# First layer's r projection as Strassen's seven products, behind q and k, with the weight-block sums formed in DRAM

## What is computed

```python
q, k, v, r, g_low = jnp.split(x @ w_in, [GLA_HK, 2 * GLA_HK, 2 * GLA_HK + GLA_HV, 2 * GLA_HK + 2 * GLA_HV], axis=-1)
log_a = jax.nn.log_sigmoid((g_low @ w_gate_up + b_gate).astype(f32)) / GLA_TAU
...
cum = jnp.cumsum(to_chunks(log_a, GLA_DK), axis=3)
q_dec = q * jnp.exp(cum); k_inv = k * jnp.exp(-cum); k_end = k * jnp.exp(total - cum)
a = jnp.where(causal, jnp.einsum('bhcid,bhcjd->bhcij', q_dec, k_inv), 0.0)
...
o = ((o - mu) * lax.rsqrt(var + LN_EPS)).reshape(B, S, GLA_HV) * norm_g.astype(f32)
y = jax.nn.silu(r.astype(f32)) * o
return y.astype(x.dtype) @ w_out
```

## Time and profile before

| What | Value |
|---|---|
| Median of 3 runs | 1132.15 us |
| The profiled execution | 1132.14 us |
| Its span | 1130.4 us |
| TensorE (PE) busy | 1120.2 us, 99% |
| Weight loads (PEld) | 994.7 us |
| VectorE (DVE) busy | 784.6 us |
| ScalarE (ACT) busy | 569.8 us |
| POOL busy | 325.6 us |
| Mean granted TensorE clock | 0.999 |

### The profile page before, as it was taken

The page is one execution under the profiler, slowest core; times in us unless marked ns, Lnnn a source line. Parts: engine busy times, 40 slices in busy tenths (PEclk is TensorE's granted clock), DMA queues, the critical chain, the costliest instruction groups (busy, mean ns, idle before and its releaser), DMA issues.

```text
span 1130.4 us, 18412 instructions
## 1 busy us (share of the span) xinstructions
PE 1120.2 (99%) x6828; PEld 994.7 (88%) x6828; DVE 784.6 (69%) x1263; ACT 569.8 (50%) x926; POOL 325.6 (29%) x215
## 2 busy tenths in 40 slices
...
GB/s 227 167 150 112 112 38 149 13 271 164 273 279 211 245 182 175 234 197 170 108 112 75 95 47 94 48 150 75 38 191 279 237 248 280 214 74 298 189 193 75
DMA packets 34459, 183.35 MB, mean 162 GB/s; under 512 B 3152, under 2 KB 7376, under 8 KB 20704
## 3 DMA queue, kind: packets, MB, share of 16 engines
...
...
## 4 chain that ended last, share of the span: by engine, by line
PE 96%; DVE 1%; issue 1%; DMA 1%; ACT 0%; POOL 0%; SPq 0%; DVEq 0%; POOLq 0%; ACTq 0%
PE bank L2057 29%; PE bank L2059 29%; PE bank L2058 29%; PE bank L2509 2%; PE bank L2493 2%; PE bank L2140 1%; PE bank L2088 1%; PE bank L2530 1%; PE bank L2529 1%; DMA s_raw<-stream 1%; PE bank L2338 1%; DVE s_w_lo L1330 1%; PE bank L2331 0%; PE bank L2346 0%; PE bank L2324 0%
## 5 line engine op out<-in xcount | busy, mean ns | idle before, releaser
L2057 PE MATMUL bank<-s_t_hi,s_w_hi 128*128 128x256 f32 (+1 forms) x832 | 264.4, 318 | 0.0
L2058 PE MATMUL bank<-s_t_lo,s_w_hi 128*128 128x256 f32 (+1 forms) x832 | 262.8, 316 | 0.0
L2059 PE MATMUL bank<-s_t_hi,s_w_lo 128*128 128x256 f32 (+1 forms) x832 | 262.8, 316 | 0.0
L1179 POOL TENSOR_TENSOR s_w_lo<-s_raw,s_w_hi 128x1024 fp32r<-128x1024 f32 x64 | 160.1, 2512 | 180.3 <-ACT s_w_hi L638 180.3
L638 ACT ACTIVATE s_w_hi<-s_raw 128x1024 fp32r<-128x1024 f32 x107 | 111.3, 1057 | 114.6 <-PE bank L2059 90.5
L2059 PEld LDWEIGHTS bank<-s_t_hi,s_w_lo 128*128 128x128 f32 x832 | 158.6, 191 | 10.2
L2057 PEld LDWEIGHTS bank<-s_t_hi,s_w_hi 128*128 128x128 f32 x832 | 158.7, 191 | 9.7 <-issue 0.2
L2058 PEld LDWEIGHTS bank<-s_t_lo,s_w_hi 128*128 128x128 f32 x832 | 158.7, 191 | 9.4
L1216 POOL TENSOR_TENSOR s_w_lo<-s_raw,s_w_hi 128x512 fp32r<-128x512 f32 x36 | 67.2, 1866 | 274.3 <-ACT s_w_hi L768 274.3
L2057 PE MATMUL bank<-s_t_hi,s_w_s_hi 128*128 128x256 f32 x432 | 122.4, 283 | 0.0
L2059 PE MATMUL bank<-s_t_hi,s_w_s_lo 128*128 128x256 f32 x432 | 122.2, 283 | 0.0
...
## 6 DMA issues: line engine op xcount, KB each, us to landing
s_raw<-stream SPq DMA_DIRECT2D x75, 1024.0 KB, 4.8
sums<-down POOLq DMA_DIRECT2D x12, 2816.0 KB, 20.9
s_more_raw<-sums SPq DMA_DIRECT2D x12, 1024.0 KB, 4.9
sums<-sums POOLq DMA_DIRECT2D x4, 2816.0 KB, 12.9
s_raw<-down SPq DMA_DIRECT2D x8, 1024.0 KB, 4.9
s_ln_gb<-ln_gb ACTq DMA_DIRECT2D x4, 1024.0 KB, 7.0
s_more_raw<-down SPq DMA_DIRECT2D x4, 1024.0 KB, 7.5
s_raw<-sums SPq DMA_DIRECT2D x4, 1024.0 KB, 4.9
```

The lines of the kernel that those rows point to most:

```text
L1179: nc.gpsimd.tensor_tensor(lo, raw_pair(SLOTS[place // 2])[:, n % 2, cols], hi.bitcast(F32), ALU.subtract).then_inc(lo_done, new)
L2057: nc.tensor.matmul(out, l_hi, r_hi, start=start, stop=False, skip_group_check=skip)
L2058: nc.tensor.matmul(out, l_hi, r_lo, start=False, stop=False, skip_group_check=skip)
L2059: return nc.tensor.matmul(out, l_lo, r_hi, start=False, stop=stop, skip_group_check=skip)
```

## The change

The order becomes v (slabs 0 to 7), q and k (8 to 15), r (16 to 29) and the output projection (30 to 37). r's 8 blocks of work become 7 products of half the tokens, half the depth and half the columns, numbered from 0; each takes two slabs, 24 matmuls. Four of the seven need sums of weight blocks: POOL issues eight transfers between its low parts of slabs 5 to 19. Sums of x are made by VectorE after the gate weights' rows, with high parts on ScalarE and low parts on VectorE behind the copies of v; a fourth one after product 2. The q and k of heads 0 and 1 are copied to SBUF by ScalarE and scaled from there. The products go into four pairs of banks, and ScalarE's copies and VectorE's additions put r's quarters together before SiLU and gain. VectorE takes r's low parts from slab 20 on. x and the layer-norm gains are loaded after product 5. Semaphores of the gate are merged.

```diff
-GLA_R = GLA_V + KD
-GLA_QK = GLA_R + KD
-GLA_OUT = GLA_QK + 2 * GLA_HEADS
+GLA_QK = GLA_V + KD
+GLA_R = GLA_QK + 2 * GLA_HEADS
+GLA_OUT = GLA_R + 2 * 7
...
+qk_raw = sb_at("qk_raw", [P, 2, 2, SEQ], F32, rg_at)
+r_ops = [halves_at(f"r_op{i}", [P, KD // 2, SEQ // 2], at_, at_ + 4 * KB)
+         for i, at_ in enumerate((h_at, h_at + 8 * KB, gb_at))]
...
 MIDDLE = P // 2 - 1
-EARLY_R = 3
+EARLY_QK = 3
+R_BANKS = {"x": (0, 1), "y": (4, 5), "z": (6, 7), "w": (2, 3)}
+R_QUARTERS = ((0, 0), (1, 0), (0, 1), (1, 1), (2, 1), (3, 1), (2, 0), (3, 0))
...
+        if GLA_R <= n < GLA_OUT:
+            p = (n - GLA_R) // 2
+            if p in SUM_READY:
+                sp.wait_ge(r_blocks, 16 * SUM_READY[p])
+            array, which = SOURCES[p]
+            sp.dma_start(raw_pair(slot).rearrange("p a c -> p (a c)"), a["r_" + array][which]).then_inc(raw_full[slot], 16)
+            continue
...
+    for i in range(3):
+        act.wait_ge(r_op_sum, i + 1)
+        nc.scalar.activation(r_ops[i]["hi"][:, :, :], r_ops[i]["sum"][:, :, :], ACT.Copy).then_inc(r_op_hi, 1)
     act.wait_ge(low_done, 1)
...
-    for n in range(GLA_R, GLA_R + EARLY_R):
+    def copy_qk(hd, is_k):
+        act.wait_ge(slab_done, GLA_QK + 2 * hd + is_k + 1)
+        nc.scalar.activation(qk_raw[:, hd, is_k, :], bank[4 + 2 * hd + is_k][:, :], ACT.Copy).then_inc(qk_copied, 1)
+    for n in range(GLA_QK, GLA_QK + EARLY_QK):
         split_hi(n + RING)
-    act.wait_ge(centred_cum, 1)
+    for hd in range(2):
+        for is_k in range(2):
+            copy_qk(hd, is_k)
+    split_hi(GLA_QK + EARLY_QK + RING)
+    act.wait_ge(gate_steps, 1)
...
-                split_hi(n + RING)
-        for t in range(TILES):
-            if t < TILES - 1:
-                act.wait_ge(tok_done[1], half * (TILES - 1) + t + 1)
-            else:
-                act.wait_ge(slab_done, GLA_R + (half + 1) * (KD // 2))
-            nc.scalar.activation(g_rg[:, t, half * HALF:(half + 1) * HALF],
-                                 bank[4 - 4 * half + t][:, :], ACT.Silu).then_inc(tok_out[1], 1)
-    for n in range(GLA_QK, GLA_OUT - 1):
-        split_hi(n + RING)
+    def r_split(first, end):
+        for slab in range(first, end):
+            split_hi(GLA_R + slab)
+    def r_done(p):
+        act.wait_ge(slab_done, GLA_R + 2 * p + 2)
+    def r_copy(b, quarter):
+        t, half = R_QUARTERS[quarter]
+        nc.scalar.activation(g_rg[:, t, half * HALF:(half + 1) * HALF], bank[R_BANKS[b][t % 2]][:, :],
+                             ACT.Copy).then_inc(r_copied, 1)
+    def r_silu(quarter):
+        t, half = R_QUARTERS[quarter]
+        act.wait_ge(r_merged, quarter + 1)
+        nc.scalar.activation(g_rg[:, t, half * HALF:(half + 1) * HALF], g_rg[:, t, half * HALF:(half + 1) * HALF],
+                             ACT.Silu).then_inc(tok_out[1], 1)
+    r_split(0, 5)
+    r_done(0)
+    act.wait_ge(qk_scaled, 6)
+    r_copy("x", 0)
+    r_copy("x", 1)
+    r_split(5, 8)
+    r_silu(0)
+    r_silu(1)
+    r_split(8, 9)
+    r_done(2)
+    act.wait_ge(r_op_sum, 4)
+    nc.scalar.activation(r_ops[0]["hi"][:, :, :], g_rg[:, 2:4, 0:HALF].rearrange("p t (k c) -> p t k c", k=2),
+                         ACT.Copy).then_inc(r_op_hi, 1)
+    r_copy("y", 4)
+    r_copy("y", 5)
+    r_split(9, 11)
+    r_done(3)
+    r_copy("x", 2)
+    r_copy("x", 3)
+    r_split(11, 14)
+    for n in range(GLA_OUT, GLA_OUT + 2):
+        split_hi(n)
+    r_silu(2)
+    r_silu(3)
+    r_done(5)
+    act.dma_start(h[:, :, :], a["x"].rearrange("(t p) d -> p t d", p=P)).then_inc(h_full, 16)
+    load_gb(0)
+    act.wait_ge(r_op_lo, 4)
+    r_copy("x", 6)
+    r_copy("x", 7)
+    r_silu(4)
+    r_silu(5)
+    split_hi(GLA_OUT + 2)
+    r_silu(6)
+    r_silu(7)
     def ke_tile_out(t):
         act.wait_ge(ke_turned, t + 1)
...
     nc.gpsimd.memset(keep[:, :].rearrange("p (t i) -> p t i", i=P)[:, :, 0:1], 0.0).then_inc(consts, 1)
     pool.wait_ge(lo_done, RING)
+    def r_block_sum(step):
+        to, array, which = SUM_STEPS[step]
+        if step:
+            pool.wait_ge(r_blocks, 16 * step)
+        if step % 2:
+            nc.gpsimd.dma_start(a["r_sums"][to], a["r_" + array][which], accum_op=ALU.add,
+                                max_dma_last_dim=R_SUM_BYTES).then_inc(r_blocks, 16)
+        else:
+            nc.gpsimd.dma_start(a["r_sums"][to], a["r_" + array][which], max_dma_last_dim=R_SUM_BYTES).then_inc(r_blocks, 16)
     for n in range(GLA_V, GLA_R):
         split_lo(n + RING)
+        if n % 2 == 1:
+            r_block_sum(n // 2)
     pool.wait_ge(norm_full, 16)
...
+    pool.wait_ge(lo_done, GLA_OUT)
+    for quarter, (t, half) in enumerate(R_QUARTERS):
+        cols = slice(half * HALF, (half + 1) * HALF)
+        pool.wait_ge(tok_out[1], quarter + 1)
+        nc.gpsimd.tensor_tensor(g_rg[:, t, cols], g_rg[:, t, cols], norm_g[:, cols], ALU.mult).then_inc(rg_done, 1)
+        if quarter % 2 == 1:
+            split_lo(GLA_OUT + quarter // 2)
     for t in range(TILES):
         pool.wait_ge(o_stats, t + 1)
...
+    nc.vector.tensor_tensor(r1, x_half(0, LATE_TOKS), x_half(1, LATE_TOKS), ALU.subtract).then_inc(r_op_sum, 1)
+    dve.wait_ge(r_op_sum, 1)
+    nc.vector.tensor_tensor(r2, r1, x_half(0, EARLY_TOKS), ALU.subtract).then_inc(r_op_sum, 1)
+    dve.wait_ge(r_op_sum, 2)
+    nc.vector.tensor_tensor(r4, r2, x_half(1, EARLY_TOKS), ALU.add).then_inc(r_op_sum, 1)
+    for t in range(2):
+        ks = slice(2 * t, 2 * t + 2)
+        last = nc.vector.tensor_tensor(g_rg[:, 2 + t, 0:HALF].rearrange("p (k c) -> p k c", k=2), x_t[:, ks, EARLY_TOKS],
+                                       x_t[:, ks, LATE_TOKS], ALU.subtract)
+    last.then_inc(r_op_sum, 1)
+    dve.wait_ge(r_op_sum, 4)
+    def r_op_low(i, src):
+        nc.vector.tensor_tensor(r_ops[i]["lo"][:, :, :], src, r_ops[i]["hi"][:, :, :].bitcast(F32),
+                                ALU.subtract).then_inc(r_op_lo, 1)
+    for i in range(3):
+        dve.wait_ge(r_op_hi, i + 1)
+        r_op_low(i, r_ops[i]["sum"][:, :, :])
     dve.wait_ge(low_part, 1)
     nc.vector.tensor_tensor(g_part[0:GLA_RANK, :], bank[0][LOW:LOW + GLA_RANK, :], g_part[LOW:LOW + GLA_RANK, :],
                             ALU.add).then_inc(low_sum, 1)
     dve.wait_ge(low_sum, 1)
...
+    def qk_of(hd, is_k):
+        return qk_raw[:, hd, is_k, :] if hd < 2 else bank[4 + 2 * (hd % 2) + is_k][:, :]
     def scale_q(hd):
-        nc.vector.scalar_tensor_tensor(out=g_q[:, hd, :], in0=bank[4 + 2 * (hd % 2)][:, :], scalar=GLA_DK ** -0.5,
+        nc.vector.scalar_tensor_tensor(out=g_q[:, hd, :], in0=qk_of(hd, 0), scalar=GLA_DK ** -0.5,
                                        in1=g_q[:, hd, :], op0=ALU.mult, op1=ALU.mult).then_inc(qk_scaled, 1)
...
-        for i, scale_part in enumerate((scale_k, scale_q) if hd == GLA_HEADS - 1 else (scale_q, scale_k)):
-            dve.wait_ge(slab_done, GLA_QK + 2 * hd + i + 1)
+        for i, scale_part in enumerate((scale_q, scale_k)):
+            if hd < 2:
+                dve.wait_ge(qk_copied, 2 * hd + i + 1)
+            else:
+                dve.wait_ge(slab_done, GLA_QK + 2 * hd + i + 1)
             scale_part(hd)
...
+    def r_low(first, end):
+        for slab in range(first, end):
+            split_low(GLA_R + slab)
+    def r_add(quarter, first, second, op):
+        t, half = R_QUARTERS[quarter]
+        out = g_rg[:, t, half * HALF:(half + 1) * HALF]
+        first, second = (out if b is None else bank[R_BANKS[b][t % 2]][:, :] for b in (first, second))
+        nc.vector.tensor_tensor(out, first, second, op).then_inc(r_merged, 1)
+    dve.wait_ge(lo_done, GLA_R + RING)
+    r_low(4, 7)
+    dve.wait_ge(slab_done, GLA_R + 4)
+    dve.wait_ge(r_copied, 2)
+    r_add(0, None, "z", ALU.add)
+    r_add(1, None, "z", ALU.add)
+    r_low(7, 10)
+    dve.wait_ge(r_op_hi, 4)
+    r_op_low(0, g_rg[:, 2:4, 0:HALF].rearrange("p t (k c) -> p t k c", k=2))
+    r_low(10, 14)
+    dve.wait_ge(slab_done, GLA_R + 10)
+    dve.wait_ge(r_copied, 6)
+    r_add(2, "y", None, ALU.subtract)
+    r_add(3, "y", None, ALU.subtract)
+    dve.wait_ge(r_copied, 8)
+    r_add(4, None, "x", ALU.subtract)
+    r_add(5, None, "x", ALU.subtract)
+    dve.wait_ge(slab_done, GLA_R + 14)
+    r_add(6, None, "w", ALU.add)
+    r_add(7, None, "w", ALU.add)
...
-    def r_free(half, t):
-        if half == 0:
-            pe.wait_ge(tok_out[0], TILES + t + 1)
-        else:
-            pe.wait_ge(abs_done, t + 1)
-            pe.wait_ge(min_done, t + 1)
-    token_major(1, GLA_R, lambda half, t: 4 - 4 * half + t, r_free, beside=gate_up)
...
-        for is_k in ((1, 0) if hd == GLA_HEADS - 1 else (0, 1)):
-            n = GLA_QK + 2 * hd + (1 - is_k if hd == GLA_HEADS - 1 else is_k)
+        for is_k in range(2):
+            n = GLA_QK + 2 * hd + is_k
             pe.wait_ge(lo_done, place_of(n) + 1)
             if hd < 2:
-                pe.wait_ge(tok_out[1], 2 * hd + is_k + 1)
+                pe.wait_ge(tok_out[0], TILES + 2 * hd + is_k + 1)
```

(43 more changed lines are left out.)

94 lines of the change are left out of this document (40 added, 54 removed).

## The result

The changed kernel took 1133.82 us (median of 20 runs, 1133.01 to 1134.79), the kernel before beside it 1132.14 (20 runs, 1131.91 to 1132.62): ratio 1.0014, 95% interval 1.0008 to 1.0021. So it is slower by 1.7 us, where 0.24 us less was forecast. 5.4 us of matmuls did go; three waits and a stretch of slower matmuls took back more than that. The profiled execution took 1133.82 us with a span of 1132.1, 1.7 above the span before.

What follows compares the result with a forecast made beforehand. TensorE, busy 99% of the span, was taken to bound the kernel. The terms -5.44 + 2.3 + 0.9 + 1.4 + 0.6 = -0.24 took 1132.14 us to 1131.9 us, range 1129.0 to 1136.5.

Steps and rivals of the forecast that it cites:

- Removed: r's matmuls on TensorE: 168 instead of 8 slabs of 24, so 24 fewer at 0.2267 us each, -5.44 us.
- Gate rows: Before the gate matmuls: x sums' high and low parts delay the low rows, so TensorE waits, +2.3 us.
- VectorE and POOL take turns: At the q/k scalings: POOL's low parts hold the shared port, so the second product waits for scalings, +0.9 us.
- bound of 3.2: Upper bound of the second product's wait, if four POOL low parts get in among the scalings: 3.2 us.
- The lock: VectorE and POOL's SBUF port pair is held exclusively for a whole instruction; with shared bandwidth the 0.9 us would be nothing.
- Weight-block sums: POOL's eight 1 MB transfers, taken as 6 us plain and 9 accumulating, delay nothing TensorE needs: 0 us charged.
- POOL's backlog: After the products: POOL's gain multiplications and low parts, 19.8 us from T - 8.5, delay o's first variance, +0.6 us.
- Tail: After the last product: ScalarE copies k out only behind two SiLUs, so the state updates start later, +1.4 us.
- Later stages: Down projections' first loads are issued later, x and layer-norm gains load later; TensorE waits for neither: 0 us charged.
- raw loads late: Rival, chance 0.2: late loads hold ScalarE's last high parts, k copy at T + 5; 1134.8 us, or 1138 at 9.2 us loads.
- transfers hold POOL's queue: Rival, chance 0.1: slow accumulating transfers delay POOL's low parts; 1134.5 us, or 1147 or more at unscaled transfer times.
- own upper figure, 1133.8: Top of the sum's own range: four low parts among the scalings and POOL a low part later, 1133.8 us.

Runs made afterwards that it cites:

- sixth kernel: Changed kernel with the x sums' high and low parts moved out of the gate's chain and q/k scalings in head order 2, 0, 3, 1: 1129.48 us, ratio 0.9979.
- 12: Changed kernel with ten unread filler matmuls ahead of the gate and q/k scalings in head order 2, 0, 3, 1: 1132.21 us, ratio 0.9999.
- 5: Changed kernel with only the q/k scalings reordered to heads 2, 0, 3, 1, product 1 waiting for nine: 1134.18 us, ratio 1.0016.
- first four kernels: Changed kernel with, separately: ten filler matmuls before the gate (1134.71 us), four (1135.02), an extra VectorE subtraction there (1134.98), x sums out of the gate's chain (1132.53).
- tenth kernel: The sixth kernel without POOL's eight block-sum transfers, all products loading plain weight blocks (wrong numbers in four): 1128.18 us, ratio 0.9964.

## Why the prediction was wrong

The forecast was 0.24 us less, the result 1.68 more. The step that failed is the gate's: the prediction priced the gap there at its 2.3 us of waiting alone, and behind it the granted clock fell to 0.50, which cost TensorE 1.70 us. Next come the raw loads beside the transfers, priced at nothing, and the number of low parts among the scalings. Term by term:

- **Removed, -5.44: right.** T = 136.21 in the sixth kernel against 141.79 before.
- **Gate rows, +2.3: right.** 2.39 measured, released by the low rows as written. But the prediction gave the gap only its length. **This is the step that failed in the profile:** the granted clock behind the gap, named in the last sentence as what no row of before can price, cost another 1.70 us. Fillers (12 against 5) took it away.
- **VectorE and POOL take turns: mechanism right, the wait hidden or mis-sized.** Exponentials at 87.77 (87.6 forecast), though POOL's low part of slab 15 met the centring (4.31 us, 2.29 before) and not a scan, and the last scaling done at 106.6 (106.8 forecast). Product 1 waited 0 where 0.9 was forecast, because the drop had delayed TensorE past it. Without a drop at the gate it is 2.4 to 2.5 in the profiles of the first four kernels, with four low parts in place of three, the case the prediction kept as its bound of 3.2. For the changed kernel itself this is inferred: no profile of it without the drop was taken, but its time then would be 1132.14 - 5.44 + 2.39 + 2.5 + 1.3 = 1132.9 (turn_y(0) waits for nothing in those four profiles), and its lowest were 1133.01 and 1133.09. So by this estimate an execution without the drop is no faster than the kernel before either, and there the failed term is this one: 2.5 instead of 0.9. By the same estimate the drop's 1.70 us make an execution only about 0.9 longer (1133.82 against 1132.9), because they cover this wait. The lock was right with it: a port shared in bandwidth would not have turned an operation on 128x4 from 0.16 into 2.23 us. The x sums met POOL too, which the prediction left out: those of 128x1024 took 3.3 us each, all five 13.4 instead of about 5, and TensorE waited for none of them.
- **Weight-block sums, 0: wrong by 1.3.** The four plain transfers landed in 5.4 to 7.6 us (6 taken), the four accumulating ones, all later than forecast, in 9.9 to 13.3 (9 taken). POOL waited 1.0, 4.3 and 0.7 us for them, which cost nothing. What the step left out is the raw loads beside the last of them: the high parts of slabs 24 and 28 waited 2.7 and 3.3 us, and by the tenth kernel, beside the sixth, that is 1.3 us of the time. It reaches TensorE through POOL's backlog, two steps below, and is not to be added to it.
- **Tail, +1.4: right.** 1.32 measured (143.14 - 140.45, less the 1.37 of before).
- **POOL's backlog, +0.6: mechanism right, size off.** 1.45 (0.02 ahead at the updates, 1.43 late at turn_y(0)). POOL started at T - 6.9, not T - 8.5, for the raw loads just named; its 19.3 us of work (19.8 forecast) then end at T + 12.4.
- **Later stages, 0: nearly.** The span grew by 1.7, and 1.43 of that stood already at turn_y(0).

In the profile: -5.44 + 2.39 + 1.70 + 1.32 + 1.45 = +1.42, with 0.25 left in later stages, to 1133.82. The rival "raw loads late" has a part in it, as POOL's start and not as a k copy at T + 5; "transfers hold POOL's queue" has none: no low part came too late behind a transfer. The range, 1129.0 to 1136.5, held the time, but its bounds were worked out for other causes, so that is luck and bears out no step. The prediction's own upper figure, 1133.8, does not follow from its terms: 3.2 in place of 0.9 alone makes its sum 1134.2.
